# A decoder block with routed experts on one core: the router on the residual sum, and the first unit's weights, lists and rows fetched by the mixer's program

## The reference, cut to what matters

```python
h = rmsnorm(x, norm_mix_g);  proj = h @ w_in            # 1024 tokens x 1024
y_rnn, y_pool, y_mem = ...                              # RG-LRU, pooling, cross-attention
x = x + concat(y_rnn, y_pool, y_mem) @ w_out
hx = rmsnorm(x, norm_ffn_g)                             # x * rsqrt(mean(x*x) + eps) * g
logits = hx @ w_router + b_router                       # 32 experts
top_vals, top_idx = top_k(logits, 4);  gates = softmax(top_vals)
gu = hx[token] @ w_gu[e] + b_gu[e]                      # 1024 x 2048, each token's 4 experts
y = ((clip(up) + 1) * glu) @ w_down[e] + b_down[e]
out = rmsnorm(x + sum of gate * y, final_norm_g)
```

## Time and profile before

| | us |
|---|---|
| median of 3 runs (1742.73 to 1752.03) | 1742.83 |
| the profiled execution | 1748.18 |
| its span | 1746.5 |
| TensorE busy in the span | 1678.8 (96%) |
| mean granted clock of TensorE | 0.983 |

### The profile page before, as it was taken

The page is one execution under the profiler, slowest core; times in us unless marked ns, Lnnn a source line. Parts: engine busy times, 40 slices in busy tenths (PEclk is TensorE's granted clock), DMA queues, the critical chain, the costliest instruction groups (busy, mean ns, idle before and its releaser), DMA issues.

```text
span 1746.5 us, 29387 instructions
## 1 busy us (share of the span) xinstructions
PE 1678.8 (96%) x8625; PEld 1250.9 (72%) x8626; DVE 1300.7 (74%) x1163; ACT 1102.7 (63%) x1065; POOL 466.1 (27%) x354
## 2 busy tenths in 40 slices
PE   7999999859999999999999999999999999999997
PEld 6877788636786767888868877678666667665673
DVE  5578656566787778999878997779668768764785
ACT  5464555355676666887767876667566666653673
POOL 5000001332322325232224222225213126122254
PEclk9999999869999999999999999999999999999998
DMA  9121132468898979999989998799868798787685
GB/s 280 52 96 61 49 109 73 154 234 290 328 347 325 340 293 357 382 388 373 393 327 350 384 385 312 289 345 368 317 259 301 281 346 322 282 309 282 237 301 205
DMA packets 114174, 485.67 MB, mean 278 GB/s; under 512 B 16431, under 2 KB 29041, under 8 KB 81361
## 3 DMA queue, kind: packets, MB, share of 16 engines
q1 hardware_dynamic: 96128, 445.58, 65.9%
q0 software_dynamic: 18000, 39.49, 9.3%
HBM read 451.79 MB, written 33.23 MB: 278 GB/s over the span
## 4 chain that ended last, share of the span: by engine, by line
PE 69%; DVE 4%; issue 2%; DMA 2%; ACT 2%; POOLq 0%; ACTq 0%; DVEq 0%; POOL 0%; SPq 0%
PE ps L1818 19%; PE ps L1820 18%; PE ps L1819 18%; PE ps L1833 6%; PE ps L1871 3%; DVE w_lo L1664 3%; PE ps L1791 2%; PE ps L1841 1%; DMA raw_weights<-in_w_down 1%; ACT w_hi L1520 1%; PE ps L1896 1%; DVE raw_weights L1765 1%; DVE raw_weights L1780 0%; PE ps L1800 0%; DMA stand_in<-token_lists 0%
## 5 line engine op out<-in xcount | busy, mean ns | idle before, releaser
L1664 DVE TENSOR_TENSOR w_lo<-raw_weights,w_hi 128x2048 fp32r<-128x2048 f32 x256 | 577.1, 2284 | 131.6 <-ACT w_hi L1520 131.4
L1520 ACT ACTIVATE w_hi<-raw_weights 128x2048 fp32r<-128x2048 f32 x256 | 485.7, 1911 | 217.5 <-DMA raw_weights<-in_w_gu 107.8
L1818 PE MATMUL ps<-w_hi,xT 128*128 128x512 f32 x1024 | 415.4, 406 | 10.4 <-issue 7.5
L1819 PE MATMUL ps<-w_lo,xT 128*128 128x512 f32 x1024 | 402.3, 393 | 0.0
L1820 PE MATMUL ps<-w_hi,xT 128*128 128x512 f32 x1024 | 401.3, 392 | 0.0
L1664 DVE TENSOR_TENSOR w_lo<-raw_more,w_hi 128x2048 fp32r<-128x2048 f32 x128 | 290.1, 2285 | 29.4 <-ACT w_hi L1520 29.4
L1818 PEld LDWEIGHTS ps<-w_hi,xT 128*128 128x128 f32 x1024 | 193.7, 189 | 91.0 <-issue 44.3
L1520 ACT ACTIVATE w_hi<-raw_more 128x2048 fp32r<-128x2048 f32 x128 | 244.0, 1907 | 1.2 <-DMA raw_more<-in_w_down 1.2
L1440 POOL DMA_INDIRECT x_rows<-h_rows,next_list x33 | 77.7, 2355 | 608.4 <-issue 608.4
L1820 PEld LDWEIGHTS ps<-w_hi,xT 128*128 128x128 f32 x1024 | 193.6, 189 | 42.7
L1819 PEld LDWEIGHTS ps<-w_lo,xT 128*128 128x128 f32 x1024 | 194.2, 190 | 36.6
(11 more groups left out here) (310 smaller groups left out, 2159.6 us busy)
## 6 DMA issues: line engine op xcount, KB each, us to landing
raw_weights<-in_w_gu SPq DMA_DIRECT2D x192, 1024.0 KB, 9.3
raw_more<-in_w_gu SPq DMA_DIRECT2D x64, 1024.0 KB, 6.8
raw_weights<-in_w_down SPq DMA_DIRECT2D x64, 1024.0 KB, 9.7
raw_more<-in_w_down SPq DMA_DIRECT2D x64, 1024.0 KB, 12.1
rows<-in_x SPq DMA_DIRECT2D x12, 512.0 KB, 4.9
w_in_sb<-in_w_in SPq DMA_DIRECT2D x12, 512.0 KB, 4.3
acc_rows<-region_c SPq DMA_DIRECT2D x8, 512.0 KB, 2.6
h_rows<-region_c SPq DMA_DIRECT2D x8, 512.0 KB, 3.8
```

Of the source, the lines that this page charges most:

```text
L1520: S.activation(w_hi[:, j % RING, :], raw(j % RING), ACT.Copy).then_inc(hi_done, 1)
L1664: V.tensor_tensor(w_lo[:, j % RING, :], raw(j % RING), w_hi[:, j % RING, :].bitcast(F32), ALU.subtract).then_inc(lo_done, 1)
L1818: T.matmul(out, hi, hi_w, start=first, stop=False)
L1819: T.matmul(out, hi, lo_w, start=False, stop=False)
```

## The change

Four things, in one diff.

1. The router works on the residual sum. `transpose_x2` transposes x2 and not h2, the gain `norm_ffn_g` is multiplied into the router's weights once (a new vector `V_GFFN`), and `pick` multiplies the logits by the token's `rs2`. With it the order in the loop changes: `transpose_x2(t-1)` at k = 3 and `route(t-1)` at k = 6 of `out_project(t)` (2 and 5 for tile 7), `rank(t-1)` after it; on VectorE `pick` and `place` are those of tile t-1, `place` stands between `residual` and `norm`, and `mixed_lo_tile` ahead of `largest`; on ScalarE `x2T_evac(t-1)` stands ahead of `exps`, and in tile 7 ahead of the root.
2. The first unit's work moves into the mixer block: SP issues pieces 0 to 3 before the stores of tile 7, then bias rows and pieces 4 and 5; ScalarE makes the high parts of pieces 0 to 3, VectorE the low parts of 0 (before it copies the unit table), 1 and 2; POOL loads the lists and issues the gather of unit 0.
3. Products of the identity (`keep_active`) stand ahead of TensorE's waits: 4, 4, 6, 5, 16 and 24 in the mixer, 8 in the experts block.
4. The mixer block ends without POOL's drain.

```diff
-        block = ctx.enter_context(nc.Block("mixer"))
+        block = ctx.enter_context(nc.Block("mixer", no_gpsimd_drain=True))
...
             for t in range(TT):
+                if t == TT - 1:
+                    sp.wait_ge(out_ready, TT)
+                    for j in range(RAW):
+                        load_piece(sp, dram, shared, 0, j)
                 sp.wait_ge(h2_done, t + 1)
...
-            sp.wait_ge(out_ready, TT)
-            for j in range(RAW):
+            sp.wait_ge(const_set, 12)
+            load_bias(sp, scratch, shared, 0)
+            for j in range(RAW, RING):
                 load_piece(sp, dram, shared, 0, j)
...
+            pool.wait_ge(scattered, 16 * TT * TOPK)
+            pool.dma_start(next_list[:, :], scratch["table"][0:P, :]).then_inc(next_in, 16)
+            pool.dma_start(next_tail[:, :], scratch["table"][P:UNIT, :]).then_inc(next_in, 16)
+            pool.wait_ge(logits_ready, TT)
+            pool.wait_ge(h2_done, TT)
+            pool.wait_ge(zero_out, 32)
+            for i in range(2):
+                pool.wait_ge(stored[i], 32 * (TT // 2))
+            pool.wait_ge(next_in, 32)
+            pool.indirect_dma_start(
+                out=first_rows[:, :], out_offset=None, in_=scratch["h2"],
+                in_offset=bass.IndirectOffsetOnAxis(ap=next_list[:, 0:1], axis=0)).then_inc(first_rows_in, 16)
...
-            def shared_attention(t):
-
+            for t in range(TT):
                 if t + AHEAD < TT:
                     probT_evac(t + AHEAD)
-                if t + 1 < TT:
                     mixed_hi_tile(t + 1)
-                if t >= 2:
-                    gate_exp(t - 2)
+                if t:
+                    x2T_evac(t - 1)
                 if t + AHEAD + 1 < TT:
                     exps(t + AHEAD + 1)
+                if t:
+                    gate_exp(t - 1)
                 act.preload_act_table(ACT.Sqrt)
...
+                if t == TT - 1:
+                    x2T_evac(t)
                 act.wait_ge(ms2_done, t + 1)
...
+            V.tensor_tensor(w_r_sb[:, :, :], w_r_sb[:, :, :],
+                            vec[:, V_GFFN:V_GFFN + KT].unsqueeze(2).broadcast_to([P, KT, E]), ALU.mult).then_inc(router_scaled, 1)
             dve.wait_ge(gain_in, 16)
             for t in range(TT):
                 if t + AHEAD < TT:
                     o_evac(t + AHEAD)
-                if t >= 2:
-                    pick(t - 2)
+                    mixed_lo_tile(t + 1)
                 if t + AHEAD + 1 < TT:
                     largest(t + AHEAD + 1)
-                if t + 1 < TT:
-                    mixed_lo_tile(t + 1)
-                if t + AHEAD + 1 < TT:
                     divide(t + AHEAD + 1)
+                if t:
+                    pick(t - 1)
                 residual(t)
+                if t:
+                    place(t - 1)
                 norm(t)
-                if t >= 2:
-                    place(t - 2)
...
             V.tensor_copy(ucol[:, 9:10], end[:, E - 1:E]).then_inc(ucol_done, 1)
+            first_split_lo(0)
             dve.wait_ge(utab_ready, 1)
             link(V.tensor_copy(utab[0:1, :], bank(6)[0:1, 0, :]))
+            for j in range(1, RAW - 1):
+                first_split_lo(j)
...
-                    if k == KT // 2:
-                        if t + AHEAD + 1 < TT:
-                            scores(t + AHEAD + 1)
-                        transpose_h2(t - 1)
+                    if k == (3 if t < TT - 1 else 2):
+                        transpose_x2(t - 1)
+                    if k == KT // 2 and t + AHEAD + 1 < TT:
+                        scores(t + AHEAD + 1)
+                    if k == (6 if t < TT - 1 else 5):
+                        route(t - 1)
...
+            def keep_active(n):
+
+                for _ in range(n):
+                    T.matmul(bank(0)[:, 0, 0:P], ident[:, :], ident[:, :], start=True, stop=True)
+
             first_out_project()
             for t in range(1, TT):
                 out_project(t)
-                if t >= 2:
-                    rank(t - 2)
-                route(t - 1)
-            transpose_h2(TT - 1)
-            rank(TT - 2)
+            keep_active(4)
+            transpose_x2(TT - 1)
+            keep_active(4)
             route(TT - 1)
+            keep_active(6)
             rank(TT - 1)
+            keep_active(5)
...
+            keep_active(16)
             pe.wait_ge(ucol_done, 1)
...
+            keep_active(24)
...
-            pe.wait_ge(x_in, 32)
+            for _ in range(8):
+                T.matmul(ps[:, 7, 0:P], ident[:, :], ident[:, :], start=True, stop=True)
+            pe.wait_ge(first_rows_in, 16)
             transpose_x(0)
             transpose_x(1)
```

More of the change, by code:

```diff
@@ L1223, in route @@
                 else:
[L1224 removed]
+                    pe.wait_ge(router_scaled, 1)
                 for k in range(KT):
[L1226 removed]
+                    last = T.matmul(bank(6)[:, 0, 0:E], x2T[t % 2][:, k, :], w_r_sb[:, k, :],
                                     start=(k == 0), stop=(k == KT - 1))
@@ L1272, in load_piece, with load_bias @@
         sp.dma_start(slot.rearrange("p (k n) -> p k n", k=2), w[:, k:k + 2, :]).then_inc(signal, 16)
+def load_bias(sp, scratch, shared, expert):
+    at = bass.ds(expert, 1) if not isinstance(expert, int) else slice(expert, expert + 1)
+    for q in range(4):
+        sp.dma_start(shared["bias_rows"][32 * q + 1:32 * q + 1 + BIAS_ROWS, :],
+                     scratch["bias"][at, q].rearrange("a r n -> (a r) n")).then_inc(shared["bias_in"], 16)
 def expert_phase(nc, dram, scratch, shared, out):
@@ L1381, in _ @@
             n = n_units(sp)
-            def load_bias(expert):
-                for q in range(4):
-                    sp.dma_start(bias_rows[32 * q + 1:32 * q + 1 + BIAS_ROWS, :],
-                                 scratch["bias"][bass.ds(expert, 1), q].rearrange("a r n -> (a r) n")).then_inc(bias_in, 16)
-            first = unit_value(sp, 0, 0, E - 1)
-            load_bias(first)
-            for p in range(RAW, RING):
-                load_piece(sp, dram, shared, first, p)
             with sp.Fori(0, n) as u:
@@ L1452, in gather @@
                 per_tails(pool, tails, lambda t: rest(t * TAIL))
+            def gather(tails):
+                pool.indirect_dma_start(
+                    out=x_rows[:, :], out_offset=None, in_=scratch["h2"],
+                    in_offset=bass.IndirectOffsetOnAxis(ap=next_list[:, 0:1], axis=0)).then_inc(x_in, 16)
+                gather_tail(tails)
             def lists_next(u):
@@ L1546, in _ @@
             act.preload_act_table(ACT.Gelu_apprx_sigmoid)
-            for j in range(RAW):
-                act.wait_ge(raw_in[j], 16)
-                split_hi(j)
+            round_bias(1)
             x_hi(0, 0)
@@ L1673, in _ @@
             dve.sem_inc(y_tail_folded, 1)
-            for j in range(RAW):
-                split_lo(j, 0)
+            split_lo(RAW - 1, 0)
             x_lo(0, 0)
```

125 lines of the change are left out of this document (69 added, 56 removed).

## The result

| | kernel before | changed kernel |
|---|---|---|
| median of 20 runs, us | 1747.38 | 1758.57 |
| lowest, highest | 1741.75, 1759.78 | 1747.34, 1769.05 |
| ratio, 95% interval | | 1.0043 (1.0024 to 1.0062) |

By the ratio, which is formed from the single runs, the change costs 7.5 us; the two medians lie further apart, 11.2 us. In a later comparison the same kernel stood at 1.0018 (0.9991 to 1.0045), 3 us; one disturbed run of the kernel before (4323.87 us, of 35) is left out of it. So "within 0.5%" held and the number did not: 1738.7 was forecast from a base of 1742.83, a ratio of 0.9976, and the range ended at 1745. Times that base, the two ratios give 1750.3 and 1746.0.

What follows compares the result with a forecast made beforehand. TensorE sets the pace, so the first expert product's start decides: loop +10.95, tail -13.45, clock -1.6 sum to -4.1 us, giving 1744.1 by profile and 1738.7 for the median (from 1742.83); range 1729 to 1745.

Steps and rivals of the forecast that it cites:

- The loop: Mixer's out-projection over eight tiles: new order adds 2.45, 6.7 and 1.8 us, 10.95 in sum.
- The stall of tile 0: First tile: mixed_lo_tile ahead of largest delays exps and transposes of the probabilities, holding TensorE 2.45 us.
- The stalls of `attend`: Tiles 1 to 5: place ahead of norm delays ScalarE's evacuation, so TensorE stalls 1.25 us in each.
- The moved router, transposes and ranking: Inside the loop: router moved into the tile 1.8 us, new ranking 0.4, transposes unchanged; 2.2 of the 10.95.
- From residual to pick: Tail, last tile: pick(7) comes 5.7 us behind the last residual, with norm, transposes and router no longer in a row.
- GpSimd's chain: Tail: scatters, lists, gather's issue on POOL; done 21.0 to 25.6 us behind the last E, taken as 24.1, ending the block.
- the last E: Out-projection, tile 7: moment its last product is out and TensorE turns to what follows; 331.45 before, 342.4 forecast.
- just about hidden: First unit's gather: issued before 23.9, needed by 27.1, taking between 3.2 and 6.7 us, so costing almost no wait.
- The clock: After the block, to the first expert products: 2.4 GHz instead of 1.2 GHz, 1.6 us saved; zero the other bound.
- Rival C: Tail: POOL's chain or the gather comes last, first product at 33 instead of 29.9, time 1741.8; chance 0.12.
- B: Rival, loop: no stall, only moved router and ranking cost, 2.2 of the 10.95; time 1730; chance 0.20.
- D: Rival, tail: clock falls to 1.2 GHz and identity products become the last arrival, +9.1, time 1751.9; chance 0.06.

Runs made afterwards that it cites:

- e9: The changed kernel run once more, unaltered; 1759.97 us in its profiled execution, ratio 1.0018 to the kernel before.
- e1: The changed kernel with VectorE's old loop order (norm ahead of the placing, largest ahead of the split of mixed); ratio 1.0014 to the kernel before.
- e6: The changed kernel with all six pieces of the first expert issued only after the last scatter has landed; one profiled execution, no ratio, scatter 2.40 us.
- e7: The changed kernel with the router part alone undone, its loop as in the kernel before; ratio 1.0046 to the kernel before.
- e12: e8 with pieces 4 and 5 issued only after the first unit's rows have landed; 1739.40 us profiled, ratio 0.9957 to the kernel before.
- e8: The changed kernel with e1's order, pieces 4 and 5 after the lists, second unit's list and gather ahead of the stand-in transfers; ratio 0.9977.
- e10: e7 with pieces 4 and 5 after the lists and the second unit's list and gather ahead of the stand-in transfers; ratio 0.9999.
- e16: e12 unaltered, a second profiled execution of the same program; 1755.33 us.

## Why the prediction was wrong, step by step

**The loop** held in mechanism, and its number partly by luck. Last residual forecast at 342.6, measured 342.7 to 345.1. The best of the four, e9, is 11.05 us later than the kernel before, where 10.95 was summed, but from other terms. The stall of tile 0 is 2.4 (2.79 less the 0.42 of before, forecast 2.45). The stalls of `attend` were forecast at 1.25 in each of five tiles and cost 0.9, 4.5 in sum for 6.25. The moved router, transposes and ranking were put at 2.2 and are 3.65, by the tiles of e1 against those of the kernel before. And the loop starts later, which was put at nothing: TensorE's first `attend` behind 205 us is at 209.6 to 210.5 for 209.1, so 0.5 us in e9 and 1.4 in the others; where that comes from no run shows. What is left above e9 lies in tile 1. e1 shows VectorE's order to be the cause of the stalls, with both halves of the order undone together.

**From residual to pick** held: 5.7 forecast, 5.56.

**The step that failed is GpSimd's chain**: "taking 2.0 to 3.6 for the scatter" and from it "I take 24.1, and the block ends there". The measured time from the last scatter to the lists is 7.5 to 8.7 us, and the block ended 25.8 to 26.6 behind the last E, past the upper end of 25.6. With it fell that the gather "is issued before 23.9" and "just about hidden": it is issued at the block's end, and the transposes, forecast 27.15 behind the last E (24.1, 0.95 and 2.1), start at 31.4 in the mean, within 0.2 us of its landing. These are 4.2 of the 4.9 us that the tail is too long.

The price was read from the rows of small transfers in the kernel before, where the pieces had left; the change moves the scatter nearer to them and two more pieces ahead of it. e6 measured 2.40 without that load: the number was right for a state that the change abolishes. (The row named had landings up to 5.7; why the scatter got 3.6 of them is not said.) The trace of the kernel before had the other state as well, in windows as the earlier trace rows:

```profile
340.00:348.00 8.00, 5.54 (x24) 5.27 (x24) 5.33 (x25) 0.87 (x3) 6.04 (x7) 0.50 1.01 391
352.00:354.00 2.00, 0.00 (x0) 0.00 (x0) 1.65 (x11) 0.00 (x0) 1.69 (x2) 0.50 0.03 1
```

The scatters issued there from 340.13 to 345.24 landed in 5.6 to 6.1 us, the last one, at 353.15, in 2.1. The argument that 7.3 MB "are done by about 20" was aimed at the gather; the scatter at 14.1 lay in it, and the DMA engines were busy until about 23 (share 0.86 from 366 to 367 us, 0.48 in the next).

**The clock** failed: 1.6 was counted for 2.4 GHz after the block, and the granted clock there was 0.50 to 0.56. The condition given, "no gap in the new tail is over 2 us", did not hold either, as the late chain made one of 4.75 to 5.49. But it was not what decides: with 1.98 in that place e7 and e12 were at 1.00 for the first products and e8, e10 and e16 were not, and e6 was at 1.00 with 10.47. What sets the clock there stays open. Rival C had GpSimd's chain last, and its sign, a wait of the first transposes on the gather, was there in two of four executions; but it put the first product at 33 instead of 33.8 to 35.8, and kept the 1.6 of the clock.

**Left out of the sum**: the first unit. That GpSimd's start of the experts' part had been hidden in the time now saved was not looked at. TensorE's wait for these rows costs 0 to 4.0 us, 1.4 in the mean of four.

**And the sum**: the first product was forecast 2.5 sooner and is 4.1 later (mean 378.9), a miss of 6.6: 4.9 in the tail (34.6 behind the residual in the mean, for 29.7; 4.2 up to the transposes and 0.7 from them to the product) and 1.7 in the loop. With the 1.6 of the clock and the 1.4 of the first unit it is 9.6 us. Against the first ratio (+7.5 for -4.1) the forecast missed by 11.6, against the second by 7.2, so these 9.6 lie between. How much of a ratio is gaps, the ratios can't tell. The base was off on its own: 1742.83, the median of three runs, was 4.5 us below the median of twenty.

**B and D** fell: the loop stalls, and the clock was 1.00 from the last residual to the end of the 24 identity products, which took 5.62.

## What to carry to other kernels

A small transfer whose landing is waited for must be priced at the load it will meet, not at the load it had: 2.4 us in the quiet and 8.7 behind six 1 MiB transfers, for the same 128 entries. The trace before the change had both states here, and the row to take was the one with the load that was to come. Two good edits can spoil each other there, and what helped here was to hold back the bulk that is needed last, not to start everything sooner. When work is pulled ahead, look for what had been hidden behind the time that is saved, on the engine that nobody watches.

## What was not expected of the hardware

One program on one core varied by 14.6 us between two executions (1346.0 and 1360.6 behind the second unit's start). To see were five gaps instead of one, at unit boundaries (463, 585, 673, 934 and 1129 us in e16, of which e12 has the first), the fall of the clock behind most of them, and 36 packets of 16 KB instead of 27 on the instruction queue. The Trainium skill ("Runtime: NRT & Kernel Launch", Instruction fetch mechanics) says that a taken branch to a target outside of what is loaded makes the engine wait for a fetch; the gaps at the ends of the loop over units fit that. Why it happens in one execution and not in the next, no run here shows.
